# A one-core MoE decoder step: the transposes of one expert's activations moved into the next expert's up products, the first expert written out, and a re-ordered end

## The chip, the cores and the metric

The kernel runs on one core of a Trainium2 chip. The metric is the device time of one execution in microseconds (us); the time before is the median of three runs.

## The reference, cut to what matters

One decoder layer for a prompt of 256 tokens and 64 sample tokens (320 tokens, width 1024, float32). After the mixing part comes a mixture of 32 experts, four of them for each token, then a gated residual and a final RMS norm:

```python
def expert(args):
    xe, e = args
    hu = xe @ w_up[e] + b_up[e]                  # (slots, 1024) @ (1024, 2048)
    gate = jnp.minimum(hu[:, :D_FF], SWIGLU_LIMIT)
    lin = jnp.clip(hu[:, D_FF:], -SWIGLU_LIMIT, SWIGLU_LIMIT)
    glu = gate * jax.nn.sigmoid(SWIGLU_ALPHA * gate)
    return ((lin + 1.0) * glu) @ w_down[e] + b_down[e]   # (slots, 1024) @ (1024, 1024)
...
x = x + gt_f * moe(...)
y = rms_norm(x, g_final)
```

Each expert has 8 MB of up weights and 4 MB of down weights, and all 32 experts' weights have to come from HBM once.

## The kernel before

Each engine runs its own hand-ordered instruction list; semaphores join them (`S("name")`, `wait_ge`, `then_inc`). All on-chip data lies in one SBUF array `mem` and one PSUM array `psum` of 8 banks, so the profile shows those two names for nearly everything, and the lines tell the operations apart.

**Weights.** SyncE (SP) issues the loads. Up weights of an expert come as 4 pieces of 2 MB (`load_up`, L434) into 4 places, down weights as 4 pieces of 1 MB (`load_down`, L439) into 4 other places. There is one set of places for each kind, so a piece of expert e+1 can be issued once TensorE has counted up `piece_done` for that place with expert e. The order on the queue is: all of expert 0, up 1, and from then on up e, down e-1. The down weights of expert 31 (`load_last`, L452) go into the places of the up weights' first two pieces.

**TensorE (PE)**, in `expert(e)`, for each of the 32 experts in a hardware loop: the down products of expert e-2 (`down`, L1096; its bias L1076); the token counts of two experts read into registers; the up products of expert e over the 4 pieces (`up`, L1048; its bias L1052), in one of four sizes by token count (32, 64, 96 or 128 slots; `by_size`); the gather of expert e+1's tokens (L1008) into banks 4 and 5; the scatter of the outputs of expert e-2 for token tiles 0 and 1 (`scatter`, L1106); the transposes of expert e's activations (`turn_activations`, L1058) into banks 4 and 5, of which there are 2, 4, 6 or 8 by size; the transposes of the scatter weights (`turn_weights`, L1114) into bank 2; the scatter of tile 2. In the first two experts there is nothing to scatter, and 14 or 3 dummy products (`fill`, L517) stand in its place. `Pg` and `G` are the scatter weights before and after the transposes.

**VectorE (DVE)**: one-hot selectors for the next gather (L2143), the scatter weights (L2154), the gated activation in `swiglu` (L2172, L2173, L2176, L2179) into `gt_`, and the additions of the scattered outputs (L2205, counted by `added`). **ScalarE (ACT)**: the sigmoid (L1496), the copy of the gathered tokens (L1483), the copy of the turned weights (L1519), the copy of the turned activations into `actT` (L1510 to L1513) and of the down products into `yd` (L1530). **GpSimd (POOL)** picks the bias row (L1700, L1703).

Expert sizes in this data, in order of experts, as the counts of the L1052 and L1048 instructions show them: 96, 32, 32, 96, 64, 32, 64, 64, 32, 32, 64, 96, 64, 32, 64, 32, 32, 128, 32, 32, 32, 32, 32, 64, 64, 32, 64, 64, 32, 32, 64, 64.

**The end** (`last_expert` on PE and ACT, `finish` on DVE): down 30; transposes of expert 31's scatter weights (bank 1); down 31 in banks 6 and 7, whose start waits until ACT has copied expert 30's outputs out of those same banks (`y_copied`). Between the two halves of down 31 stand the scatter products of expert 30 (L1177, L1181). Then come the scatter products of expert 31 (sample tile L1188, prompt tiles L1193), the residual additions (L2230, L2232, L2235), per tile a sum of squares on ACT (L1546), two small steps on POOL (L1598, L1599), the scaling on DVE (L2240) and the store (L489). Tiles go in the order 2, 0, 1 (`LAST_ORDER`); the scalings all stand behind the additions of all tiles.

Of the kernel before, what the change touches and what calls it, by code (L numbers as in the profile page):

```python
# [13 lines left out]
D = 1024  # L14
# [71 lines left out]
def build(nc, a):  # L86
# [6 lines left out]
    with ctx:  # L93
# [128 lines left out]
        yd_last = at(2 * SLOT, 2, 512); G_last = at(2 * SLOT + D, NTOK)  # L222
        assert o5 + 7168 + 1536 <= WORDS, o5 + 8704
# [284 lines left out]
        def _(pe):  # L508
# [3 lines left out]

            def fill(n, bank):

                busy = at_bf(const_off["ones"], 256)
                for _ in range(n):
                    pe.matmul(psum[:, bank, 0:256], busy[:, 0:128], busy, start=True, stop=True)  # L517
# [466 lines left out]

            def gather_first():
# [13 lines left out]
                last.then_inc(S("gathered"), 1)  # L999

            def gather(i, count, turned, e=None):
# [12 lines left out]
                if count is None:  # L1014
                    products(128)
                    return
# [22 lines left out]
            def up(ig, it, slots):  # L1039
# [4 lines left out]
                for c in range(UP):  # L1044
                    pe.wait_ge(piece_in[c], 16 * (it + 1))
# [17 lines left out]
            def down(it, slots, meanwhile=None):  # L1063

                end = meanwhile is not None
# [9 lines left out]
                for u in range(2):  # L1075
                    pe.matmul(psum[0:slots, 6 + u, :], bsel_down[:, 0:slots],  # L1076
                              bparts[:, 2 * D + 512 * u:2 * D + 512 * u + 512], start=True, stop=False)
                last = [None] * DOWN
                for j in range(pieces):
                    if end and j == pieces // 2:  # L1080
                        meanwhile()
                    for u in range(2):
                        for q in range(tiles):
                            piece = q * pieces + j
                            c = piece // 2
                            if slots == 96:
                                turned = actT.rearrange("p j s -> p (j s)")[:, 0:8 * slots] \
                                    .rearrange("p (j s) -> p j s", j=KD)[:, piece, :]
                            else:
                                turned = actT[:, j, slots * q:slots * q + slots]  # L1090
# [5 lines left out]
                            last[c] = pe.matmul(psum[slots * q:slots * q + slots, 6 + u, :], turned,  # L1096
# [19 lines left out]

            def expert(e):
# [6 lines left out]
                by_size(pe, count, lambda slots: up(e, e, slots))  # L1124
# [24 lines left out]
            def expert_later(r, e, it, count_before):  # L1149
# [10 lines left out]
                turn_activations(it, SIZES[3])  # L1160
# [5 lines left out]
            def last_expert(its, count):  # L1166
# [3 lines left out]
                turn_weights(its, 1)  # L1170

                def scatter_before():

                    pe.wait_ge(S("G_ready"), its + 1)
                    pe.wait_ge(S("y_copied"), its + 1)
                    for u in range(2):
                        pe.matmul(psum[64 * u:64 * u + 64, 0, :], G[:, tok(2)], yd[:, u, :], start=True, stop=False)  # L1177
                    pe.wait_ge(S("y_gated"), 2)
                    for t in range(2):
                        for u in range(2):  # L1180
                            pe.matmul(psum[:, 2 + 2 * t + u, :], G[:, tok(t)], yd_gated[:, u, :], start=True, stop=False)  # L1181

                pe.wait_ge(S("y_copied"), its + 1)
# [1152 lines left out]
```

## Time and profile before

| | |
|---|---|
| median of 3 runs | 1298.41 us (1296.67 to 1298.94) |
| the profiled execution | 1295.37 us |
| its span, first to last instruction | 1293.6 us |
| PE busy | 1163.6 us (90%) |
| DVE, ACT, POOL busy | 375.8, 182.7, 72.0 us |
| data moved, mean rate | 467.36 MB, 361 GB/s |
| DMA queue of the weights (q1), share of 16 engines | 86.7% |
| mean granted TensorE clock | 0.970 |

PE is busy for 90% of the span and the DMA engines for 87%. Which of the two sets the time changes from stage to stage, so the shares alone do not say what an edit is worth. "Released" below means that the last product that reads a piece of weights is done.

### The profile page before, as it was taken

The numbers are of one execution on the slowest core, as the hardware profiler recorded it, in microseconds if no ns is written. First come the engines' busy times: TensorE is split into PE (matmuls) and PEld (weight loads), VectorE is DVE, ScalarE is ACT, GpSimd is POOL, SyncE is SP. The second block draws the span as 40 slices with busy tenths as digits, with TensorE's granted clock in tenths as the row PEclk, the third lists the DMA queues.
The fourth block names the chain that finished last, engine by engine and source line by source line (L and its number), as shares of the span: only waits on it lengthen the run. The fifth ranks groups of instructions, "written<-read, shape, count | busy, mean of one in ns | idle before, by whom it ended". The sixth has DMA issues, their size and how long they took to land.

```text
span 1293.6 us, 23349 instructions
## 1 busy us (share of the span) xinstructions
PE 1163.6 (90%) x8690; PEld 567.3 (44%) x8691; DVE 375.8 (29%) x819; ACT 182.7 (14%) x358; POOL 72.0 (6%) x178
## 2 busy tenths in 40 slices
PE   5999999996989999998999998999777889988986
PEld 4655447544335446443344544444223334343332
DVE  0164214848211222321222121142211221222235
ACT  3112232213010111110110110010100000110101
POOL 1010001431000000000000000000000000000001
PEclk9999999998899999998999999999879999989999
DMA  9944635883689999999999999999999999999992
GB/s 366 363 152 172 239 131 196 253 317 138 260 351 424 409 417 427 427 428 425 428 424 426 426 426 428 426 376 428 427 426 428 426 425 426 426 426 428 427 422 85
DMA packets 62481, 467.36 MB, mean 361 GB/s; under 512 B 6538, under 2 KB 24910, under 8 KB 26730
## 3 DMA queue, kind: packets, MB, share of 16 engines
q1 hardware_dynamic: 59770, 461.86, 86.7%
q10 hardware_dynamic: 2288, 4.37, 1.1%
q0 software_dynamic: 384, 0.59, 0.2%
q8 instruction: 28, 0.46, 0.1%
q14 instruction: 11, 0.09, 0.0%
HBM read 459.78 MB, written 6.42 MB: 360 GB/s over the span
## 4 chain that ended last, share of the span: by engine, by line
PE 58%; DMA 36%; DVE 2%; issue 2%; ACT 1%; POOL 0%; SPq 0%; ACTq 0%; POOLq 0%; DVEq 0%
DMA mem<-in_w_up 33%; PE psum L1048 20%; PE psum L1096 9%; PE psum L680 6%; PE psum L1106 5%; PE psum L661 3%; PE psum L1008 3%; PE psum L867 2%; PE psum L684 2%; DMA mem<-in_in_chunks 1%; PE psum L536 1%; DMA mem<-in_mod_chunks 1%; PE psum L1058 1%; PE psum L871 1%; PE psum L1052 1%
## 5 line engine op out<-in xcount | busy, mean ns | idle before, releaser
L1048 PE MATMUL psum<-mem 128*32 128x512 f32 (+2 forms) x2432 | 399.9, 628 | 74.0 <-DMA mem<-in_w_up 66.8
L1048 PEld LDWEIGHTS psum<-mem 128*32 128x32 f32 (+2 forms) x2432 | 133.7, 123 | 330.3 <-issue 203.4
L1096 PE MATMUL psum<-mem 128*32 128x512 f32 (+3 forms) x1024 | 207.8, 594 | 0.0
L2172 DVE TENSOR_SCALAR mem<-psum 128x256 f32<-128x256 f32 (+3 forms) x32 | 19.2, 601 | 542.6 <-PE psum L1052 542.6
L1106 PE MATMUL psum<-mem 128*128 128x512 f32 x360 | 143.1, 608 | 3.3 <-DVE mem L2173 2.2
L1096 PEld LDWEIGHTS psum<-mem 128*32 128x32 f32 (+3 forms) x1024 | 93.3, 127 | 87.4 <-issue 61.2
L2205 DVE TENSOR_TENSOR mem<-mem,psum 128x1024 f32<-128x1024 f32 (+1 forms) x90 | 94.1, 1045 | 95.8 <-PE psum L1106 95.8
L680 PE MATMUL psum<-mem 128*128 128x512 f32 x192 | 84.2, 595 | 0.0
L1008 PEld LDWEIGHTS psum<-mem 128*128 128x128 bf16 x2232 | 74.7, 99 | 19.4 <-issue 19.1
L1496 ACT ACTIVATE mem<-mem 128x256 f32<-128x256 f32 (+3 forms) x32 | 17.9, 561 | 451.0 <-DVE mem L2172 451.0
L1008 PE MATMUL psum<-mem 128*128 128x64 bf16 (+1 forms) x2232 | 78.4, 196 | 0.0
L1106 PEld LDWEIGHTS psum<-mem 128*128 128x128 f32 x360 | 49.0, 171 | 51.9 <-issue 47.3
L1700 POOL CAST mem<-mem 128x128 bf16 (+1 forms) x33 | 10.7, 324 | 937.5 <-PE psum L1096 894.2
L680 PEld LDWEIGHTS psum<-mem 128*128 128x128 f32 x192 | 36.0, 190 | 43.7 <-issue 43.6
L2143 DVE TENSOR_SCALAR mem<-mem 128x128 bf16<-128x128 f32 (+1 forms) x99 | 22.2, 281 | 69.2 <-issue 69.2
L1513 ACT COPY mem<-psum 128x256 f32<-128x256 f32 (+2 forms) x29 | 14.0, 484 | 189.1 <-PE psum L1096 189.1
L661 PE MATMUL psum<-mem 128*128 128x320 f32 x128 | 36.7, 447 | 2.1 <-DMA mem<-in_in_chunks 2.1
L1246 ACT COPY mem<-psum 128x320 f32<-128x320 f32 (+9 forms) x65 | 25.0, 395 | 95.4 <-PE psum L680 68.1
L1519 ACT COPY mem<-psum 128x320 f32<-128x320 f32 x32 | 13.7, 428 | 155.9 <-PE psum L1106 147.7
L536 PE MATMUL psum<-mem 128*32 128x128 f32 x768 | 25.0, 286 | 7.8 <-DMA mem<-in_mod_chunks 6.9
L1530 ACT COPY mem<-psum 128x1024 f32<-128x1024 f32 x31 | 31.5, 1018 | 0.0
L661 PEld LDWEIGHTS psum<-mem 128*128 128x128 f32 x128 | 25.0, 197 | 13.1 <-DMA mem<-in_in_chunks 2.2
(279 smaller groups left out, 803.4 us busy)
## 6 DMA issues: line engine op xcount, KB each, us to landing
mem<-in_w_up SPq DMA_DIRECT2D x128, 2048.0 KB, 22.3
mem<-in_w_down SPq DMA_DIRECT2D x128, 1024.0 KB, 15.9
mem<-in_mod_chunks SPq DMA_DIRECT2D x12, 2048.0 KB, 12.3
mem<-in_in_chunks SPq DMA_DIRECT2D x8, 2048.0 KB, 9.9
mem<-in_out_chunks SPq DMA_DIRECT2D x2, 2048.0 KB, 10.0
mem<-in_x_prompt ACTq DMA_DIRECT2D x2, 1024.0 KB, 6.9
mem<-in_state_ret SPq DMA_DIRECT2D x4, 512.0 KB, 8.7
mem<-in_state_mlstm_c SPq DMA_DIRECT2D x4, 512.0 KB, 7.7
```

Of the source, the lines that this page charges most:

```text
L536: last = pe.matmul(psum[32 * t:32 * t + 32, bank, 0:128], cT[:, k, :], w[:, k, 128 * t:128 * t + 128], start=(k == 0), stop=False)
L661: last = pe.matmul(psum[:, q % BANKS, 0:NTOK], w[:, k, 128 * m:128 * m + 128], hT[:, k, :], start=(k == 0), stop=(k == KD - 1))
L680: last = pe.matmul(psum[:, q % BANKS, :], hT[:, k, tok(t)], w[:, k, :], start=(k == 0), stop=(k == KD - 1))
L684: last = pe.matmul(psum[64 * u:64 * u + 64, q % BANKS, 0:256], hT[:, k, tok(t)], w[:, k, 256 * u:256 * u + 256], start=(k == 0), stop=(k = ...
L867: last = pe.matmul(psum[:, 6 + u, :], hT[:, k, tok(t)], w[:, k, :], start=(k == 0), stop=(k == KD - 1))
L1008: last = pe.matmul(psum[:, 4 + k // 4, 128 * (k % 4):128 * (k % 4) + slots], h2p[:, part, t, dealt(k)], P[:, t, 0:slots], start=(part == 0 ...
L1048: last = pe.matmul(out, xg[:, 2 * c + h, cols], moving, start=(c + h == 0), stop=False)
L1096: last[c] = pe.matmul(psum[slots * q:slots * q + slots, 6 + u, :], turned, place(c, 2, D)[:, piece % 2, 512 * u:512 * u + 512], start=(j = ...
L1106: last = pe.matmul(out, G[:, tok(t)], yd[:, u, :], start=True, stop=True)
L1246: act.copy(*pairs[-1]).then_inc(S("evacuated"), 1)
L1530: act.copy(yd.rearrange("p u n -> p (u n)"), flat(6, D)).then_inc(S("y_copied"), 1)
L2205: TT(v, v, src, ALU.add).then_inc(S("added"), 1)
```

## The change

1. `turn_activations` moves. The transposes of expert e-1's activations are now issued inside expert e's `up`, ahead of its fourth piece, and there are always 8 of them, whatever the size. Counts of `act_ready` and `act_turned` start one higher. ACT copies them out behind the copies of the turned weights and of the down products, one expert later than before. The gather of expert e+1 waits for that copy (`actT_ready`), as banks 4 and 5 are shared.
2. The first expert (`expert_first`) is written out ahead of the loop, which now runs from 1. Its counts are read into registers in `gather_first`, ahead of the last 8 gather products. The dummy products `fill` are gone.
3. Expert 31's activations are turned between the loop and down 30, and ACT copies them into a buffer of their own (`actT_last`, in the place of up piece 2). Down 31 goes to banks 4 and 5 and runs in one piece; it no longer waits for `y_copied`. The scatter products of expert 30 stand behind it, and prompt tile 1 is multiplied after tile 0 is finished, into banks 6 and 7.
4. On DVE the scalings are put between the additions: add tile 0, scale tile 2, add tile 1, scale tile 0, scale tile 1. The load of the final norm's gains is issued before down 31 is done.

```diff
             def gather_first():
...
                     for t in range(NT):
+                        if part == 2 and t == NT - 1:
+                            pe.wait_ge(S("counts_ready"), 1)
+                            first_counts = count_at(1), count_at(2)
                         pe.wait_ge(S(f"part{part}"), t + 1)
...
-            def up(ig, it, slots):
+            def up(ig, it, slots, turn_before=False):
...
                 for c in range(UP):
+                    if turn_before and c == UP - 1:
+                        turn_activations(it - 1)
                     pe.wait_ge(piece_in[c], 16 * (it + 1))
...
-            def turn_activations(it, slots):
-                pe.wait_ge(S("act_ready"), it + 1)
-                for j in range(KD * slots // 128):
+            def turn_activations(it):
+                pe.wait_ge(S("act_ready"), it + 2)
+                for j in range(KD):
...
+            def expert_first(count, count_next):
+                by_size(pe, count, lambda slots: up(0, 0, slots))
+                gather(1, count_next, 1)
+                pe.wait_ge(S("gate_ready"), 1)
+                pe.wait_ge(S("lin_clipped"), 1)
+                pe.nop().then_inc(S("scattered"), 1)
+                pe.nop().then_inc(S("scattered"), 1)
+                pe.wait_ge(S("added"), 1 + CLEARED)
+                turn_weights(0, 2)
+                pe.nop().then_inc(S("scattered"), 1)
...
-                by_size(pe, count, lambda slots: up(e, e, slots))
+                by_size(pe, count, lambda slots: up(e, e, slots, True))
                 gather(e + 1, count_next, e + 1, e)
...
                     pe.nop().then_inc(S("scattered"), 1)
                     pe.nop().then_inc(S("scattered"), 1)
-                    with pe.If(e < 1):
-                        fill(14, 6)
-                    with pe.Else():
-                        fill(3, 6)
-                pe.wait_ge(S("xg_ready"), e + 3)
-                by_size(pe, count, lambda slots: turn_activations(e, slots))
                 pe.wait_ge(S("added"), 3 * e + 1 + CLEARED)
                 turn_weights(e, 2)
...
             def last_expert(its, count, acts):
...
+                by_size(pe, count, lambda slots: down(its - 1, slots, True, acts))
+                pe.wait_ge(S("G_ready"), its + 1)
+                pe.wait_ge(S("y_copied"), its + 1)
...
+                samples(G, yd, True)
+                pe.wait_ge(S("y_gated"), 2)
+                prompt(0, G, yd_gated, True)
                 pe.wait_ge(S("G_ready"), its + 2)
+                samples(G_last, yd_last, False).then_inc(S("last_scattered"), 1)
                 pe.wait_ge(S("y_gated"), 4)
+                prompt(0, G_last, yd_last_gated, False).then_inc(S("last_scattered"), 1)
+                prompt(1, G, yd_gated, True)
+                prompt(1, G_last, yd_last_gated, False).then_inc(S("last_scattered"), 1)
...
-            with pe.Fori(0, NE) as e:
+            expert_first(*gather_first())
+            with pe.Fori(1, NE) as e:
                 expert(e)
+            turn_activations(NE - 1)
             by_size(pe, count_at(NE - 1), lambda slots: down(NE - 2, slots))
...
# ACT
             def expert(r, e, it, count, count_next):
                 take_up(r * (NE + 1) + e, it, count, count_next)
                 copy_weights(it)
-                by_size(act, count, lambda slots: copy_turned(it, slots, True))
+                down_before(it)
+                act.copy(yd.rearrange("p u n -> p (u n)"), flat(6, D)).then_inc(S("y_copied"), 1)
+                by_size(act, count, lambda slots: copy_turned(it, slots, actT))
...
# DVE, finish
+                add_last(0)
+                dve.wait_ge(S("gfin_in"), 16)
+                scale(0)
+                add_last(1)
+                scale(1)
+                scale(2)
```

## Rows read from the trace of the kernel before

**Rows 1.** The page: rate of the DMA in 40 slices of the span

```profile
GB/s 366 363 152 172 239 131 196 253 317 138 260 351 424 409 417 427 427 428 425 428 424 426 426 426 428 426 376 428 427 426 428 426 425 426 426 426 428 427 422 85
```

**Rows 2.** The chain that ended last, late in the loop: start, us, what

```profile
1214.78 3.68 PE psum L1048 x16
...
1244.30 3.65 PE psum L1048 x16
```

**Rows 3.** Windows: length, busy per engine, PEclk, DMA share, GB/s

```profile
308.00:332.00 24.00, 18.02 (x154) 9.95 (x158) 14.91 (x44) 8.05 (x11) 0.00 (x0) 0.78 0.01 3
...
355.00:360.00 5.00, 4.21 (x35) 2.44 (x37) 0.85 (x3) 1.20 (x3) 0.00 (x0) 0.88 0.07 29
440.00:442.00 2.00, 1.91 (x9) 0.65 (x10) 0.85 (x3) 1.49 (x3) 0.60 (x2) 1.00 0.43 94
856.00:860.00 4.00, 4.00 (x41) 1.10 (x35) 1.59 (x6) 1.93 (x2) 0.53 (x2) 1.00 0.26 55
```

**Rows 4.** SP's queue: first issues of weight loads behind the first two pauses

```profile
331.92 33.39 SPq L434 DMA_DIRECT2D mem<-in_w_up  x8
...
359.87 5.45 SPq L434 DMA_DIRECT2D mem<-in_w_up  x4
```

**Rows 5.** Timeline, from the first gather to the first up products

```profile
317.61 0.62 PE L996 MATMUL psum<-mem 128*128 128x128 bf16 x8 [0.22 <-DVE mem L2089]
...
318.27 0.69 DVE L2255 COPY mem<-psum 128x512 f32<-128x512 f32 x1 [0.72 <-PE psum L996]
...
321.81 0.87 PE L1048 MATMUL psum<-mem 128*32 128x512 f32 x1 [3.58 <-issue]
324.24 22.64 PE L1048 MATMUL psum<-mem 128*32 128x512 f32 x188 [1.56 <-issue]
```

**Rows 6.** Windows around the first products, for the granted clock (PEclk)

```profile
318.00:322.00 4.00, 0.42 (x6) 0.17 (x3) 2.92 (x13) 1.87 (x2) 0.00 (x0) 1.00 0.03 8
...
324.00:329.00 5.00, 4.76 (x24) 1.16 (x28) 2.51 (x7) 0.00 (x0) 0.00 (x0) 0.51 0.02 5
...
353.00:356.00 3.00, 3.00 (x16) 2.39 (x15) 0.67 (x3) 0.00 (x0) 0.00 (x0) 0.50 0.65 273
```

**Rows 7.** Timeline from the end of up 0 to behind up 1

```profile
350.86 0.96 DVE L2179 TENSOR_TENSOR mem<-mem 128x768 f32<-128x768 f32 x1
352.49 2.94 PE L517 MATMUL psum<-mem 128*128 128x256 bf16 x14 [2.31 <-issue]
...
357.72 7.07 PE L1048 MATMUL psum<-mem 128*32 128x512 f32 x64 [0.79 <-ACT mem L1519]
...
367.98 0.50 PE L517 MATMUL psum<-mem 128*128 128x256 bf16 x3 [0.76 <-issue]
```

**Rows 8.** The chain that ended last: the activations of a 128-slot expert turned

```profile
851.40 0.95 PE psum L1058 x8
```

**Rows 9.** The same chain from down 30 on

```profile
1255.79 7.14 PE psum L1096 x31
...
1265.29 0.38 PE psum L1076
...
1269.32 0.86 PE psum L1177 x4
1270.18 3.63 PE psum L1181 x8
...
1278.58 1.48 PE psum L1188 x4
...
1281.52 1.22 DVE mem L2232
...
1284.02 1.16 ACT mem L1546 x2
...
1287.08 1.28 POOL mem L1598
...
1289.03 1.29 DVE mem L2240
```

More of the change, by code:

```diff
@@ L983, in _, with count_at @@
             turn_rows(2)
+            def count_at(i):
+                where = slice(i, i + 1) if isinstance(i, int) else bass.ds(i, 1)
+                return pe.value_load(counts_i[0:1, where], min_val=0, max_val=NTOK)
             def gather_first():
@@ L1015, in gather @@
                     products(128)
+                    return
+                if e is None:
+                    with pe.If(count <= 64):
+                        products(64)
+                    with pe.Else():
+                        products(128)
                     return
@@ L1061, in turn_activations, with down @@
                 last.then_inc(S("act_turned"), 1)
-            def down(it, slots, meanwhile=None):
-                end = meanwhile is not None
+            def down(it, slots, end=False, acts=actT):
+                first = 4 if end else 6
                 def place(c, *shape):
@@ L1095, in down @@
                                     pe.wait_ge(piece_in[UP + c], 16 * (it + 2))
-                            last[c] = pe.matmul(psum[slots * q:slots * q + slots, 6 + u, :], turned,
+                            last[c] = pe.matmul(psum[slots * q:slots * q + slots, first + u, :], turned,
                                                 place(c, 2, D)[:, piece % 2, 512 * u:512 * u + 512],
@@ L1164, in expert_later, with last_expert @@
                 by_size(pe, count_before, lambda slots: down(it - 1, slots))
-            def last_expert(its, count):
+            def last_expert(its, count, acts):
                 pe.wait_ge(S("G_ready"), its + 1)
@@ L1170, in last_expert, with samples @@
                 turn_weights(its, 1)
-                def scatter_before():
-                    pe.wait_ge(S("G_ready"), its + 1)
-                    pe.wait_ge(S("y_copied"), its + 1)
+                by_size(pe, count, lambda slots: down(its - 1, slots, True, acts))
+                pe.wait_ge(S("G_ready"), its + 1)
+                pe.wait_ge(S("y_copied"), its + 1)
+                def samples(weights, rows, first):
                     for u in range(2):
[L1177 to L1181, printed above, removed]
@@ L1183, in last_expert, with prompt @@
-                pe.wait_ge(S("y_copied"), its + 1)
-                by_size(pe, count, lambda slots: down(its - 1, slots, scatter_before))
+                        if not first:
+                            pe.wait_ge(S("y_copied"), its + 2 + u)
+                        last = pe.matmul(psum[64 * u:64 * u + 64, 0, :], weights[:, tok(2)], rows[:, u, :],
+                                         start=first, stop=not first)
+                    return last
+                def prompt(t, weights, rows, first):
+                    for u in range(2):
+                        last = pe.matmul(psum[:, (2, 6)[t] + u, :], weights[:, tok(t)], rows[:, u, :],
+                                         start=first, stop=not first)
+                    return last
@@ L1185, in last_expert @@
+                samples(G, yd, True)
+                pe.wait_ge(S("y_gated"), 2)
+                prompt(0, G, yd_gated, True)
                 pe.wait_ge(S("G_ready"), its + 2)
-                for u in range(2):
-                    pe.wait_ge(S("y_copied"), its + 2 + u)
-                    last = pe.matmul(psum[64 * u:64 * u + 64, 0, :], G_last[:, tok(2)], yd_last[:, u, :], start=False, stop=True)
-                last.then_inc(S("last_scattered"), 1)
+                samples(G_last, yd_last, False).then_inc(S("last_scattered"), 1)
@@ L1190, in last_expert @@
                 pe.wait_ge(S("y_gated"), 4)
-                for t in range(2):
-                    for u in range(2):
-                        last = pe.matmul(psum[:, 2 + 2 * t + u, :], G_last[:, tok(t)], yd_last_gated[:, u, :], start=False, stop=True)
-                    last.then_inc(S("last_scattered"), 1)
+                prompt(0, G_last, yd_last_gated, False).then_inc(S("last_scattered"), 1)
+                prompt(1, G, yd_gated, True)
+                prompt(1, G_last, yd_last_gated, False).then_inc(S("last_scattered"), 1)
@@ L1562, in _ @@
             copy_weights(0)
-            by_size(act, count, lambda slots: copy_turned(0, slots, False))
             act.nop().then_inc(S("y_copied"), 1)
-            with act.Fori(1, NE) as e:
+            by_size(act, count, lambda slots: copy_turned(0, slots, actT))
+            with act.Fori(1, NE - 1) as e:
                 expert(0, e, e, count_at(e + 1), count_at(e + 2))
@@ L2246, in _ @@
             dve.nop().then_inc(S("added"), CLEARED)
+            dve.nop().then_inc(S("act_ready"), 1)
             dve.memset(counts[:, 0:1], 0.0)
```

67 lines of the change are left out of this document (34 added, 33 removed).

## The prediction

> **What bounds the kernel now.** I read the page first. Its rate row [rows 1] is ragged over the first 12 of 40 slices, which are the mixing part that the change does not touch. From slice 13 on (about 390 us) it stands at 409 to 428 GB/s but for one slice, the 376 of slice 27. That is a stream of weights which hardly pauses, so in the expert part the time is that of the DMA stream: its start, its pauses, and what is left to do when it has ended.
>
> The chain that ended last says the same late in the loop [rows 2]: TensorE starts the products on an expert's fourth up piece at 1214.78 and on the next one's at 1244.30, 29.5 us later, and between them stands the landing of weights. 12.58 MB in 29.5 us is 426 GB/s, the full rate. An edit inside such an iteration is worth nothing as long as TensorE is back in time.
>
> Then I looked for the pauses of the stream [rows 3]. There are four behind the last piece of expert 0's weights: 308 to 332 (24 us, 3 GB/s), 355 to 360 (29 GB/s instead of 426, so 4.7 us lost), 440 to 442 (94 GB/s, 1.6 us lost) and 856 to 860 (55 GB/s, 3.5 us lost). In each the queue had nothing to do because TensorE had not released a piece. The first ends at the issue of 331.92, when the first piece of expert 0 is released, the second at 359.87, with the first piece of expert 1 [rows 4]. These two are what parts 1 and 2 of the change can reach. Behind up 31 the stream has only the last down weights to bring, and the end is a chain of PE, DVE, ACT and POOL [rows 9], which parts 3 and 4 reach.
>
> **Part A, the start of up 0.** The last 8 gather products start at 317.61, and DVE's copy of the tokens ends at 318.27 + 0.69 = 318.96. The first up product starts only at 321.81, 2.85 us later, with "issue" as releaser, and the second at 324.24, behind another 1.56 us of "issue" [rows 5]. In the first gap stand two register loads, the entry of the loop, a branch, and the choice of size. The change takes the loads and the loop entry out of it. No row prices them apart. From below: the branches and jumps alone make up the gap, gain 0; indeed the loads may hold back the last 8 gather products, which had only 0.22 us of waiting. From above: all 2.85 us. I take 1.5. The second gap I leave as it is, for the same products stand behind the same kind of branch.
>
> The gap has a second price. The granted clock is 1.00 over 318 to 322 and 0.51 over 324 to 329 [rows 6], 1.2 instead of 2.4 GHz, after TensorE had been busy for 0.42 of 4.00 us. 24 products in 4.76 us at the low level are about 2.4 us more than they take at the high one. With the idle shortened to about 2 us before the first product, whether the clock falls is open: it was still full at 322. I count half, 1.2 us (ends: 0 and 2.4). Part A gives 1.5 + 1.2 = 2.7 us (0 to 5.3), and as the queue waits for this very release, the stream is earlier by all of it.
>
> **Part B, from up 0 to the first release of up 1.** Before, TensorE waits 2.31 us for "issue", runs 14 dummy products, turns and reaches up 1 at 357.72 [rows 7]. Now the dummies and the turn are gone. What must be waited for is `added`, which DVE counts behind its last activation step, at 350.86 + 0.96 = 351.82. With half a microsecond for the three weight transposes that is done near 352.6 (three at the 0.12 of [rows 8], and a handover). From there it could go on at once, but now the loop is entered, with code that has not run yet: the same loop entry, two loads and choice of size that part A sheds. By the gap of part A, 2.85 us, up 1 starts at 355.5, 2.2 us earlier than before. But the dummies were what kept TensorE at work: even with them the clock was at 0.50 over 353 to 356 [rows 6], and it was back in time for up 1 at 357.72. Without them up 1 meets the low level, and its first piece (a quarter of the 7.07 us of [rows 7], 1.77 us) takes 3.54. So the release comes at 359.0 instead of 359.5: gain 0.5. Bounds: with an entry of no cost up 1 starts 5.1 earlier, less the 1.8 of the clock, +3.3; with the second gap of 1.56 us too, -1.1, taken as -1.5.
>
> The Trainium skill (TensorE: Matmul & The Clock Gate, the part on the clock gate) calls the low clock the default and says that it is activity which lifts it; it speaks against taking the dummy products away. The row of 353 to 356 agrees. If the clock never fell, part B would be 2.2 us instead of 0.5.
>
> **Part C, the turn inside the up products.** Work moves and grows: always 8 transposes where there were size / 16. 8 take 0.95 us [rows 8], 0.12 us each. Over 16 experts of 32 slots, 12 of 64 and 3 of 96 that is 96 + 48 + 6 = 150 more, 18 us in all. They cost nothing where TensorE waits for the fourth piece anyway, as it does wherever the pattern of [rows 2] holds: the third piece's products, 3.68 at 64 slots, and 0.95 us fit into the 4.9 us between two pieces. If that cover went, each would cost its 0.12.
>
> It counts where TensorE leads, from up 1 on, and the pause at 440, which ends with a down piece released in expert 4, measures it. Up to there 8 turns each come into up 1, 2 and 3: +2.85. Behind up 1 go a gap of 0.76 and 3 dummies of 0.50 [rows 7]; behind up 1, 2 and 3 go 2 + 2 + 6 turns, 1.2. That is 2.85 - 0.76 - 0.50 - 1.2 = +0.4, and the pause grows by it: loss 0.5 (0, where it is hidden, to 2, if ACT's copy of the turned activations also holds up the gather; the fourth piece's products, 1.77 us and more, cover it otherwise). What is queued behind `act_ready` on TensorE is the rest of the up products, but the activations are ready an iteration before. The pause at 856 has one turn of 0.95 moved from behind the products to inside them, hence no change.
>
> **Part D, the end.** All of it hangs on the landing that starts the products at 1244.30. 8 transposes instead of 4 before down 30: +0.5. Down 30 ended at 1255.79 + 7.14 = 1262.93, and down 31 waited for ACT's copy until 1265.29 [rows 9]. Now it follows the weights' transposes: 1262.93 + 0.5 + 0.5, and 0.8 for the choice of size, as in the gap of 0.76 [rows 7]: 1264.8, gain 0.5. It runs in one piece, 0.38 + 7.14 = 7.5 us like down 30, to 1272.3. Then come the samples of expert 30 (0.86) and prompt tile 0 (half of 3.63, 1.81), and the second samples start at 1275.0. Before, L2232 started 1281.52 - 1278.58 = 2.94 behind that point; so now at 1277.9, ending at 1279.2. Scaling tile 2 waits for 1.16 on ACT and 0.8 to 1.95 on POOL; with 0.8 it runs 1281.2 to 1282.5. Prompt tile 1's 3.63 us of products end at 1281.3, so its addition, like L2232 some 1.22, runs 1282.5 to 1283.7. Its square takes 1.16. From the start of POOL's last step to that of the last scaling lie 1289.03 - 1287.08 = 1.95, and the scaling takes 1.29: 1288.1, with handovers 1288.3. Before it ended at 1289.03 + 1.29 = 1290.3. Gain 2.0 (1.0 if down 31 gains nothing and the handovers cost 0.5 more; 3.2 if POOL's last step is as short as 0.7). What is late next is POOL behind the last square.
>
> **Sum.** 2.7 + 0.5 - 0.5 + 2.0 = 4.7 us. The profiled execution took 1295.37 us, of which 1293.6 are the span; it would take 1290.7. The median of the three runs, 1298.41, lies 3.0 above the profiled one, and I carry the difference over: 1293.7.
>
> **The rivals.**
> *The start gives nothing back.* Part A's gap is branches and jumps, the clock falls as before, and the new loop entry eats part B. Then A is 0, B is 0 and the rest 1.5: 1296.9. For it: "issue" is named for the whole gap, no load is seen in it. Against: the same branches cost 2.31 us at 352.49 without a register load and 0.76 an iteration later [rows 7], so a gap is not of one size, and the loads' share of 2.85 is not nothing.
> *The clock stays up.* With shorter idle both times, TensorE is at 2.4 GHz in up 0 and up 1: A is 3.9 to 5.3, B 2.2, D 2.0, less 0.5: about 8 us, 1290.4. For it: the full level at 318 to 322. Against: the fall at 353 after only 2.3 us of idle.
> *Slower: the loop is met cold.* Written out, the first expert warms none of the loop's code, so the entry cost is paid twice: both gaps of [rows 5], 2.85 + 1.56, fall between 352.6 and the second product of up 1, and the rest of up 1 and its 8 transposes run at the low level. First release 357.0 + 3.54 = 360.9, a loss of 1.4; the rest of up 1 loses 3 us more, which all go into the pause at 440, with 2 of part C at its upper bound; A gives 0 and the end 2.0. Loss 4.4: 1302.8. It decides when up 1's first release is later than 361 and the pause at 440 longer than 5 us. Against: up 1 is the first of size 32, so its code ran for the first time at 357.72 too, as one group of 64 without a gap [rows 7].
> The Trainium skill (Runtime: NRT & Kernel Launch, instruction fetch mechanics) says that a taken branch whose target is not in the engine's present window makes it fetch, and stall. By that rule this last rival's two gaps would come. No row here names a fetch.
>
> **How the numbers follow.** The case of the sum has 0.50, the start that gives nothing 0.24, the clock that stays up 0.18, the cold loop 0.08. A change of 0.2%, 2.6 us, is about what a measurement of this kernel can tell from none. The first case runs from 1290.5 to 1297.0, mostly beyond 2.6 us, with 0.05 of its 0.50 inside; the second lies within it; the third is faster. The cold loop splits 0.07 slower and 0.01 same. Faster 0.63 and, with 0.04 of the second case that gains over 2.6 by the end alone, 0.67; same 0.26; slower 0.07. The range leaves out the cold loop and the outer halves of the others: 1289.5 to 1297.8.
>
> **What would show each step.** A: the first up product near 320.3, the issue at 331.92 now near 329.2. B: the second issue near 356.7 (359.87 less 0.5 and A), the granted clock at half when up 1 starts. C: 8 turns ahead of each fourth piece, the pause at 440 about 0.5 longer, 29.5 us from fourth piece to fourth piece unchanged. D: 44.0 us from the fourth piece's products of expert 31 to the end of the last scaling, instead of 1290.3 - 1244.3 = 46.0. The whole would be wrong if a new pause of the stream appears between 440 and 560, or if the gather waits for ACT.

## The result, and the profile after

The changed kernel takes 1309.82 us (median of 4 runs, 1308.26 to 1312.82), the kernel before beside it 1298.55 (4 runs, 1296.67 to 1298.94): a ratio of 1.0106, 95% interval 1.0083 to 1.0129. It is 11.3 us slower; the prediction had 4.7 us faster and a range that ended at 1297.8. The profiled execution took 1308.91 us, its span 1307.1, which is 13.5 us more than before.

The rate row of the page answers to [rows 1]:

```profile
GB/s 368 368 136 190 216 130 195 291 278 138 265 255 385 377 416 405 425 426 429 427 426 426 401 428 423 427 393 428 426 427 427 427 427 425 424 426 426 426 425 146
```

Slices 12 to 14, about 359 to 457 us, were at 351, 424 and 409 GB/s; now they are at 255, 385 and 377. The loss is there, at the start of the expert part. To the right of it the row is nearly what it was.

The timeline of TensorE from the first gather on answers to [rows 5, 7]: start, us, what, and in brackets the idle time ahead of it and what ended it.

```profile
318.08 0.62 PE L998 MATMUL psum<-mem 128*128 128x128 bf16 x8 [0.37 <-issue]
319.69 20.81 PE L1059 MATMUL psum<-mem 128*32 128x512 f32 x192 [0.99 <-DVE mem L2295]
340.28 0.86 PE L1063 MATMUL psum<-mem 128*32 128x512 bf16 x12
341.07 2.28 PE L1011 MATMUL psum<-mem 128*128 128x64 bf16 x72
345.19 0.62 PE L1124 MATMUL psum<-mem 128*128 128x128 f32 x3 [1.84 <-DVEq L2227]
352.86 7.33 PE L1059 MATMUL psum<-mem 128*32 128x512 f32 x48 [7.05 <-issue]
360.12 1.22 PE L1070 MATMUL psum<-mem 128*128 128x128 f32 x8
361.27 1.93 PE L1059 MATMUL psum<-mem 128*32 128x512 f32 x16
363.01 0.40 PE L1063 MATMUL psum<-mem 128*32 128x512 bf16 x4
369.49 1.25 PE L1011 MATMUL psum<-mem 128*128 128x64 bf16 x20 [6.07 <-issue]
374.71 2.88 PE L1011 MATMUL psum<-mem 128*128 128x64 bf16 x52 [3.98 <-issue]
381.41 0.96 PE L1124 MATMUL psum<-mem 128*128 128x128 f32 x3 [3.82 <-issue]
383.83 1.06 PE L1088 MATMUL psum<-mem 128*96 128x512 bf16 x2 [1.46 <-issue]
```

Up 0 (L1059 here is L1048 of before) starts 0.99 us behind the gather and runs as one group of 192: both gaps of [rows 5] are down to this one. Then, from the moment the loop is entered at expert 1, there are five waits named "issue" (the engine waited for nothing that the profile shows), 7.05 + 6.07 + 3.98 + 3.82 + 1.46 = 22.4 us. One of them, the 3.98, stands in the middle of 72 gather products that have nothing between them but each other. Before, the same stretch (from the end of expert 1's gather to down 0) held 2.31 + 0.76 and some 2 us more, of which 1.74 stood ahead of down 0:

```profile
371.43 0.60 PE L1076 MATMUL psum<-mem 128*96 128x512 bf16 x2 [1.74 <-issue]
```

So the last of the five waits, 1.46, is not new; the other four are new or several times longer.

The queue of the weight loads answers to [rows 4]:

```profile
325.09 38.64 SPq L435 DMA_DIRECT2D mem<-in_w_up  x8
389.90 10.63 SPq L440 DMA_DIRECT2D mem<-in_w_down  x4
...
356.72 4.00 SPq L435 DMA_DIRECT2D mem<-in_w_up  x3
```

(The last line is from a closer window, within the group of 8.) The first release is at 325.09 instead of 331.92, 6.8 us earlier; expert 1's first is at 356.72 instead of 359.87, 3.2 us earlier; but the first down piece of expert 0 is at 389.90, where it was 375.64. In 33 us TensorE went from 3.2 us ahead to 14.3 us behind. Windows answer to [rows 3, 6] (columns as there):

```profile
318.00:322.00 4.00, 2.94 (x32) 1.42 (x36) 2.88 (x13) 1.87 (x2) 0.00 (x0) 1.00 0.02 4
324.00:329.00 5.00, 5.00 (x52) 1.86 (x48) 2.89 (x7) 0.00 (x0) 0.00 (x0) 1.00 0.58 180
353.00:356.00 3.00, 3.00 (x16) 0.65 (x17) 0.00 (x0) 0.00 (x0) 0.00 (x0) 0.50 0.00 0
...
378.00:389.00 11.00, 6.13 (x12) 2.61 (x13) 1.28 (x6) 0.65 (x2) 0.00 (x0) 0.69 0.06 22
450.00:460.00 10.00, 9.64 (x59) 3.72 (x60) 3.84 (x9) 1.44 (x2) 0.53 (x2) 1.00 0.58 216
```

The granted clock stays at its upper level in up 0 (52 products in 5.00 us where there were 24 in 4.76) and is at the lower one at the start of up 1. The stream stands from 378 to 389 (22 GB/s) and runs at half its rate between 450 and 460 (216 GB/s, 4.9 us lost).

The chain that ended last, late in the loop and from the last up piece on, answers to [rows 2, 8, 9]:

```profile
1232.64 3.68 PE psum L1059 x16
...
1262.18 3.65 PE psum L1059 x16
...
1272.99 1.15 PE psum L1070 x8
...
1282.14 0.33 PE psum L1088
...
1292.33 1.03 PE psum L1195 x4
...
1294.81 1.23 DVE mem L2262
...
1301.90 0.19 POOL mem L1628
...
1302.76 1.29 DVE mem L2272
```

Fourth piece to fourth piece is 29.5 us, unchanged. Expert 31's fourth piece is met at 1262.18, 17.9 us later than before. From there to the end of the last scaling it takes 1304.05 - 1262.18 = 41.9 us instead of 46.0, so the new end gives 4.1 back: 17.9 - 4.1 = 13.8, close to the span's 13.5. The stream's own account gives the 17.9: expert 1's release came 3.2 us earlier; at 427 GB/s the 137 GB/s over 378 to 400 are 14.9 us lost; and from 400 to 1240 us it loses 13.2 us instead of 7.3. That is 14.9 + 5.9 - 3.2 = 17.6.

### The profile page after: what moved, and what is told of

It is laid out like the page before. It is cut to its first block, busy times and chain, and to the rows that moved or that the text cites. A ratio compares the mean times of both kernels' runs of the same rounds, so it can differ in the third digit from the quotient of the medians.

```text
span 1307.1 us, 23471 instructions
## 1 busy us (share of the span) xinstructions
PE 1179.1 (90%) x8821; PEld 582.9 (45%) x8824; DVE 375.7 (29%) x819; ACT 184.8 (14%) x357; POOL 70.7 (5%) x178
## 4 chain that ended last, share of the span: by engine, by line
PE 61%; DMA 32%; issue 3%; DVE 2%; ACT 1%; POOL 0%; SPq 0%; ACTq 0%; POOLq 0%; DVEq 0%
DMA mem<-in_w_up 30%; PE psum L1059 20%; PE psum L1106 10%; PE psum L675 6%; PE psum L1116 5%; PE psum L1011 3%; PE psum L656 3%; PE psum L862 2%; DMA mem<-in_mod_chunks 2%; PE psum L679 2%; PE psum L1070 1%; PE psum L531 1%; PE psum L1124 1%; PE psum L1088 1%; PE psum L866 1%
## 5 line engine op out<-in xcount | busy, mean ns | idle before, releaser
L1059 PE MATMUL psum<-mem 128*32 128x512 f32 (+2 forms) x2432 | 391.8, 611 | 57.6 <-DMA mem<-in_w_up 48.1
L1059 PEld LDWEIGHTS psum<-mem 128*32 128x32 f32 (+2 forms) x2432 | 125.9, 122 | 293.6 <-issue 199.1
L1106 PEld LDWEIGHTS psum<-mem 128*32 128x32 f32 (+3 forms) x1024 | 97.7, 128 | 83.8 <-issue 52.0
L1116 PEld LDWEIGHTS psum<-mem 128*128 128x128 f32 x360 | 50.0, 171 | 50.8 <-issue 44.3
L675 PEld LDWEIGHTS psum<-mem 128*128 128x128 f32 x192 | 36.0, 190 | 43.7 <-issue 43.6
L1070 PEld LDWEIGHTS psum<-mem 128*128 128x128 f32 x256 | 33.7, 208 | 27.6 <-issue 27.6
L1070 PE MATMUL psum<-mem 128*128 128x128 f32 x256 | 39.8, 300 | 0.0
L1511 ACT ACTIVATE mem<-mem 128x256 f32<-128x256 f32 (+3 forms) x32 | 17.9, 560 | 141.3 <-DVE mem L2202 141.3
```

The source lines that it names most:

```text
L675: last = pe.matmul(psum[:, q % BANKS, :], hT[:, k, tok(t)], w[:, k, :], start=(k == 0), stop=(k == KD - 1))
L1059: last = pe.matmul(out, xg[:, 2 * c + h, cols], moving, start=(c + h == 0), stop=False)
L1070: last = pe.transpose(flat(4, D)[:, 128 * j:128 * j + 128], gt_.rearrange("p u (w i h) -> p u w h i", w=2, h=2)[:, j // 4, j // 2 % 2, j % ...
L1106: last[c] = pe.matmul(psum[slots * q:slots * q + slots, first + u, :], turned, place(c, 2, D)[:, piece % 2, 512 * u:512 * u + 512], start= ...
L1116: last = pe.matmul(out, G[:, tok(t)], yd[:, u, :], start=True, stop=True)
```

## The experiments

Theory 1 (theory F in the first expectations): the loop's code has to be fetched when it is first run. With the first expert inside the loop, part of those fetches fell into the 22 us of up 0; with the first expert written out they fall into expert 1, which is short. Rivals: the moved turn, the missing dummy products with the clock, and, for the size of a single wait, the weights' traffic that the fetch shares the DMA engines with.

**Only the first expert written out.** The kernel before, dummies and old turn kept, counts read behind the first gather as before:

```diff
+            expert_first(count_at(1), count_at(2))
-            with pe.Fori(0, NE) as e:
+            with pe.Fori(1, NE) as e:
```

> The kernel before with one edit: the first expert is written out ahead of the loop, dummies and turn kept as they were. Theory F (first fetch under load: TensorE's loop code runs for the first time while the weights stream, and each wait for code takes 4 to 7 us instead of 1.5): long 'issue' gaps behind up 0, 15 us and more in sum between 345 and 395, and the time 10 to 18 us over the kernel before. Rival T (the 8 transposes inside the up products make TensorE late): no change, within 3 us of the kernel before. Rival L (the low clock without the dummies): no change either, as the dummies are kept.

Measured: 1308.66 us (6 runs), ratio 1.0097 (1.0066 to 1.0129), 12.9 us over the kernel before on that chip (1295.72). Its timeline has 5.08 us of "issue" ahead of up 1, 4.00 and 5.64 around the gather, 1.67 and 4.14 at the dummies, 1.44 ahead of down 0, and down 0's first release at 390.37. So this one edit makes the whole loss, with the dummies in place. Its register loads still stand behind the first gather, and yet up 0 starts 1.18 us behind it, where the kernel before needs 3.58.

**Everything but that.** The changed kernel with the loop from 0, counts read in the loop, no `expert_first`, and `bsel_ready` waited for ahead of the turn:

```diff
-            expert_first(*gather_first())
-            with pe.Fori(1, NE) as e:
+            gather_first()
+            with pe.Fori(0, NE) as e:
```

> The changed kernel with the loop running from 0 again, its first expert inside it (which turns data that nobody uses in up 0; the counts are read in the loop). Turn and end stay changed, no dummies. Theory F: the gaps behind up 0 shrink to under 5 us in sum; only the turns' cost and the end's 4 us remain, so 1294 to 1300. Rivals T and L: the time stays near 1309.

Measured: 1296.19 us (10 runs), ratio 1.0003 (0.9979 to 1.0028). The waits are back near their old size (2.85 us ahead of up 1, 0.73 ahead of the weights' transposes, 1.73 ahead of down 0), and the start is slow again: 5.85 us ahead of up 0. Down 0's release is at 377.90.

**Only the rebuilt end.** The kernel before with parts 3 and 4 of the change; the turn of expert 31 stays in the loop, ACT copies it to `actT_last`:

```diff
-                last_expert(NE, count_at(NE))
+                last_expert(NE, count_at(NE), actT_last)
```

> The kernel before with the rebuilt end alone (own buffer and banks, tile by tile; 4 transposes of expert 31 in the loop as before). From the fourth up piece of expert 31 to the last scaling 46.0 us became 41.9 in the changed kernel. Expected by every theory: that gain alone, some 4.5 us (4 transposes fewer than in the changed kernel), 1293 to 1295; if instead the end only moved with the rest, no change.

Measured: 1290.62 us (10 runs), ratio 0.9950 (0.9929 to 0.9971), 5.1 us faster. From expert 31's fourth piece to the end of the last scaling it takes 41.1 us instead of 46.0. Between this kernel and the one before it lie the moved turn and the missing dummies: 5.6 us.

**The stream held ahead of expert 1.** Is a fetch slow because weights are moving? In the changed kernel SP waits ahead of expert 1's up pieces until TensorE is inside the loop's `up`:

```diff
+            sp.wait_ge(S("entered"), 1)
             load_ups(1, 1)
```

> The changed kernel, but SyncE holds back the four up pieces of expert 1 until TensorE has entered up 1 inside the loop, so that nothing streams while the loop is entered. Theory F: the gap ahead of up 1 (7.05 us of 'issue') shrinks: up 1's code is reached within 3 us of the end of the weight transposes, seen at the issue of the first piece. A rival to it, B (the number of branches and loads alone makes the gap): 7 us from the weight transposes to that issue. The time itself is longer by either, since the stream starts 20 us later.

Measured once: 1322.46 us. Nothing moved while the loop was entered, and TensorE got from the weights' transposes (end 347.2) to the count in `up`, just ahead of the first product, by 350.9: 3.7 us, nearer to theory F's 3 than to the rival's 7. The changed kernel's 7.05 reach further, to the product itself, which here waits for its weights. But the pieces then landed beside the later waits:

```profile
381.98 1.14 PE L1012 MATMUL psum<-mem 128*128 128x64 bf16 x18 [6.24 <-issue]
387.76 3.06 PE L1012 MATMUL psum<-mem 128*128 128x64 bf16 x54 [4.64 <-issue]
394.93 0.95 PE L1127 MATMUL psum<-mem 128*128 128x128 f32 x3 [4.10 <-issue]
397.33 1.06 PE L1091 MATMUL psum<-mem 128*96 128x512 bf16 x2 [1.44 <-issue]
```

The third falls where the stream was already drying up (60 GB/s over 392 to 395), so this run decided nothing on what traffic does to the later waits. The place of the hold was badly chosen: it left the traffic on most of the waits that were to be tested.

**The stream held ahead of expert 2.** The same, one line later, until TensorE has come through the loop's first pass:

```diff
             load_ups(1, 1)
+            sp.wait_ge(S("entered"), 1)
             with sp.Fori(2, NE) as e:
```

> The changed kernel, but the weight queue waits ahead of expert 2's up pieces until TensorE has come to the end of the loop's first pass (expert 1). So TensorE meets the loop's code while no weights are moving. In the changed kernel three waits named issue lie in that stretch: 6.07 us at 363.4, 3.98 us in the middle of the gather, 3.82 us ahead of the weights' transposes, 13.9 us together. Theory 1, code met for the first time costs its fetch whatever else moves: the three stay at 10 us or more together, and the stream starts again near 383, 26 us later than it did: about 1335 us. Theory 2, a fetch is slow only because it shares the DMA engines with the weights: the three shrink to under 6 us together, the stream starts again near 375, about 1327 us.

Measured: 1303.09 us in one run, then in 10 more 1304.57, ratio 1.0059 (1.0040 to 1.0078), where the changed kernel has 1.0106. Both numbers expected for the time were far too high: I had let the held pieces be 20 us late for expert 2, and they are not, since TensorE is at down 0 when they land. Timeline and window of the first run:

```profile
364.90 1.25 PE L1012 MATMUL psum<-mem 128*128 128x64 bf16 x20 [3.76 <-issue]
367.30 2.96 PE L1012 MATMUL psum<-mem 128*128 128x64 bf16 x52 [1.16 <-issue]
371.78 0.62 PE L1125 MATMUL psum<-mem 128*128 128x128 f32 x3 [1.52 <-issue]
374.36 1.02 PE L1089 MATMUL psum<-mem 128*96 128x512 bf16 x2 [1.96 <-issue]
```

```profile
356.00:371.00 15.00, 9.34 (x120) 5.83 (x112) 2.18 (x7) 1.89 (x4) 0.00 (x0) 0.77 0.03 5
```

The same four waits are 8.4 us instead of 15.3, and the three that the forecast named 6.4 instead of 13.9, nearer to theory 2's 6 than to theory 1's 10. The first two show it cleanly: with 5 GB/s moving instead of 420 (363 to 375 us in the changed kernel) they are 4.9 us instead of 10.1. The third, 1.52 instead of 3.82, is less clear, since in the changed kernel the stream was already drying up beside it (128 GB/s over 377 to 382, most of that in the first 2 us); the fourth did not shrink (1.96, and 1.46 there). As 2.7 us of waiting stood in this stretch before the change too, code met first costs 5 to 6 us here without traffic. The changed kernel has about 7 more; 5 of them are in the first two waits and are the traffic's. The wait ahead of up 1 has expert 1's pieces beside it in both kernels, and stays at 6.84. The second set of runs had 3.49, 1.48, 1.03 and 1.62 for the four, 7.6 us.

Its expectation, written before the second set:

> The changed kernel with the stream held back during the loop's first pass, once more with rounds: it was 1303.1 us in one run, 6 us under the changed kernel, with the named waits of the first pass 8.4 us instead of 15.3. Theory 1 (a fetch waits behind the weights' transfers, which costs about as much again as the fetch): ratio 1.003 to 1.007. Theory 2 (chance of one run): 1.008 to 1.012, as the changed kernel.

**The second expert written out too.**

```diff
             expert_first(*gather_first())
+            expert_second(count_at(2), count_at(3))
-            with pe.Fori(1, NE) as e:
+            with pe.Fori(2, NE) as e:
```

> The changed kernel with the second expert written out as well, the loop from 2. Theory 1, each piece of code costs its fetch when it is first run, and a short expert (32 slots) has no long products to hide it: the written second expert shows gaps like those of the changed kernel's first pass through the loop, and the loop's first pass shows them once more: 10 us or more of new gaps, of which the stream may cover a part, 1314 to 1324 us. Theory 2, the gaps are a single cost of going into a loop from code ahead of it, wherever that is: the gaps move one expert later and the time stays within 3 us of 1309.8.

Measured: 1314.51 us (4 runs), ratio 1.0133 (1.0108 to 1.0157). The chain has the waits in the written expert 1 and once more in the loop's first pass, at expert 2:

```profile
364.64 5.89 issue
370.53 2.57 PE psum L1011 x45
373.10 4.03 issue
...
406.62 11.86 issue
418.49 1.57 PE psum L1011 x13
```

So it is each copy of the code that costs, and most of it not the step into a loop. The wait ahead of up 1 is the exception: 7.05 us where up 1 is reached by entering the loop, 1.33 (ended by ACT) where expert 1 is written out and its code follows on. The DMA section of the page counts the fetches of that queue: queue, kind, packets, MB, share. First the changed kernel, then this one.

```profile
q8 instruction: 32, 0.52, 0.2%
```

```profile
q8 instruction: 37, 0.61, 0.2%
```

Packets of 16 KB each. The kernel before has 28, as have all the kernels here with one copy of the expert; with the first expert alone written out and the old end it is 33, five more. The changed kernel, whose copy has no dummies and no turn, has four more than its twin with the loop from 0, and the second copy adds five. (That q8 is TensorE's is read from this count: in the second of the pair nothing else has grown.) Between 317 us and down 0 the changed kernel has 11 of them, the kernel before 6 (both counted in windows of the DMA view), and none of the loop's comes again after its first pass. Such packets start inside or just ahead of each of the long waits: at 348 and 351 us ahead of up 1, at 364.9 and 365.5, at 372, at 378. In the kernel before, those of 325 and 338 start under the products of up 0, that of 349 under the gather and that of 355 under the dummies and the turn, where no wait shows them. A packet is itself under way for only 0.9 to 2.1 us, so most of a wait of 4 to 6 us is not the transfer. With the stream held, the two packets behind up 1 took no less time (1.85 and 2.09 us, against 1.13 and 2.03) but started 1.1 us ahead of the wait instead of 1.5 us into it; what the traffic delays is thus at least in part their start.

**Without the dummies.** The rebuilt end, old turn, no `fill`:

```diff
-                    with pe.If(e < 1):
-                        fill(14, 6)
-                    with pe.Else():
-                        fill(3, 6)
```

> The kernel before with the rebuilt end, and without the dummy products in the first two experts; the turn of the activations stays where it was. The rebuilt end alone took 1290.6 us; with the turn moved and no dummies and the loop from 0 it was 1296.2. Theory 1, the moved turn accounts for the 5.6 us: this kernel takes 1289 to 1292. Theory 2, the dummies kept the clock and covered work, and their loss accounts for it: 1294 to 1297.

Measured: 1292.78 us (11 runs), ratio 0.9974 (0.9960 to 0.9987): between the two theories, 1 to 3 us over the rebuilt end alone (0.9950 and, later, 0.9961), though the intervals overlap. Up 1 shows a likely cause: 64 products in 9.77 us at the lower clock, where they take 7.07 with dummies ahead.

**The turn alone.** The changed kernel with the loop from 0 and the dummies kept, beside the rebuilt end alone on one chip. (The edit is that of "Everything but that", and the lines of `fill` back in.)

> The changed kernel with the loop from 0 and with the dummy products kept, so that it differs from the kernel before only in the moved turn and the rebuilt end. Theory 1, the moved turn costs 3 to 5 us by itself (8 transposes of 1.15 us in each expert where TensorE leads or lags, and gaps ahead of the down products): with the rebuilt end's 5 us gained it comes out near the kernel before, 1294 to 1297 us, and above the rebuilt end alone, which runs beside it. Theory 2, it was the missing dummies and the fallen clock at expert 1 that cost it: 1290 to 1292 us, as the rebuilt end alone.

> The kernel before with the rebuilt end alone once more, on the same chip as the three others of this set, as their measure. It had a ratio of 0.995; both theories expect 0.993 to 0.997 again.

Measured: 1295.87 us (12 runs), ratio 0.9986 (0.9966 to 1.0006), against 1291.50 (12 runs), 0.9961 (0.9942 to 0.9980). The medians are 4.4 us apart, as theory 1 of these expectations has it; the intervals overlap by a little, so that the size rests on the medians and the traces. The view of TensorE's waits over 395 to 1240 us (us in all, times, longest), first with the turn moved, then with the rebuilt end alone:

```profile
PE psum L1063 <- DMA mem<-in_w_up: 43.4, 34, 3.0
PE psum L1092 <- issue: 12.0, 29, 0.7
```

```profile
PE psum L1049 <- DMA mem<-in_w_up: 67.8, 42, 3.0
PE psum L1077 <- issue: 3.0, 8, 0.5
```

TensorE's slack against the stream falls by 24 us of 68, and the choice of size ahead of the down products is now waited for in 29 experts instead of 8. Counted from the rate in windows of 10 us against 427 GB/s, the stream loses 11.5 us between 400 and 1240 with the turn moved, and 6.7 without; 9.0 and 4.8 in the pair without dummies. The pause at 440 is not where it goes in the pair with dummies (2.7 us in both).

**Loop entered early.** An attempt at a better version: the rebuilt end, and the last 8 gather products put inside the loop, so that it is entered and the counts are read while TensorE waits for VectorE.

```diff
                 count, count_next = count_at(e + 1), count_at(e + 2)
+                with pe.If(e < 1):
+                    gather_part(2, NT - 1).then_inc(S("gathered"), 1)
+                with pe.Else():
+                    pe.nop()
                 by_size(pe, count, lambda slots: up(e, e, slots))
```

> The kernel before with the rebuilt end, and the last 8 products of the first gather moved into the loop, behind the counts and ahead of the up products, under a branch for e < 1. The loop is entered and the counts are read while TensorE waits for VectorE anyway. Theory 1 (the start's gap is loop entry and register loads, and the loop's code is fetched once in this form): up 0 starts some 2 us earlier, the clock stays up, first release near 327 instead of 332, 1284 to 1288 us. Theory 2, the gap is the choice of size alone, or the branch costs as much anew: 1289 to 1292 us, as the rebuilt end alone.

> The rebuilt end with the last 8 gather products inside the loop, once more, beside the rebuilt end alone on one chip. Its trace had expert 0's first down piece released 55.9 us behind the first gather, against 58.1 with the rebuilt end alone. Theory 1, this goes through to the end: ratio 0.991 to 0.995, 1 to 3 us under the rebuilt end. Theory 2, it is given back at the pauses behind 440 and at 850, where TensorE and not the stream sets the time: within 1 us of it or above it.

Measured: 1293.00 us (12 runs), ratio 0.9971 (0.9954 to 0.9989), and in the second set 1292.24, 0.9969 (0.9950 to 0.9988), beside 0.9961 for the rebuilt end alone. The first up product still starts 3.32 us behind the gather, so loads and loop entry alone do not make that gap; the second gap is gone, and from the gather's end to down 0's release it takes 55.9 us instead of 58.1. Those 2 us do not reach the end: in the window of 850 to 860 us, where the 128-slot expert makes TensorE the bound, the stream loses 3.8 and 4.3 us, against 1.8 (and 3.1 one window later) with the end alone. Whether that is all of it stays open.

The rebuilt end alone remains the fastest kernel, 0.4 to 0.5% under the kernel before.

## Why the prediction was wrong

**The step that failed is part B**: "the loop is entered, with code that has not run yet: the same loop entry ... By the gap of part A, 2.85 us". It priced one entry. What first-run code costs is not an entry but a fetch for every 16 KB of it: 6.57 us in the chain ahead of up 1, and then 6.07, 3.98 and 3.82 us on the way to down 0, beside the 1.46 that is no longer than before. The forecast for the second release, 356.7, was met (356.72), and by accident: part A gave 4 us more than I had, and part B took 3.7 (from first to second release 31.6 us instead of 28.0) where I had it give 0.5. And I stopped the sum there. From the second release to down 0's, 33.2 us have become of 15.8: 12.6 of the 17.4 are the "issue" waits (15.3 against 2.7 before), the rest the turn of 1.2 and products that ran at the lower clock after the waits (the gather 4.1 instead of 2.3; from down 0's first product to its release 6.1 instead of 4.2). The window of 378 to 389 is my "new pause of the stream", only earlier than where I looked for it.

**The rival named for this, "the loop is met cold", had the mechanism and a fifth of its waits, and its time, 1302.8, was still 7 us short.** (By its own terms it comes to 0.4 less: 357.0 + 3.54 is 360.5, not 360.9.) Its sign, a first release later than 361, did not show, since part A's gain hid the loss. It took both gaps of [rows 5] as the whole price, 4.4 us, because those were the only cold gaps on the page. The rest of the same code was met under work, 22 us of up 0, the gather and the dummies, as the packets' starts show: covered, not free. I priced the edit by what showed, and did not ask what up 0 had been covering. I gave it 0.08; my reason against it ("up 1 is the first of size 32, so its code ran for the first time at 357.72 too ... without a gap") mistook code that had not run for code that had not been brought: the loop's last packet there starts at 355, ahead of up 1's 357.72. The Trainium skill (Runtime: NRT & Kernel Launch, instruction fetch mechanics) says of a taken branch outside the present window that its page must be fetched before execution goes on. The run with two written experts agrees for code met first behind a choice of size (5.89 and 11.86 us, with packets starting in both); its 4.03 us stand between two products without a branch, and that rule does not give them. The section's further statement that only two blocks are held does not fit: the six or seven blocks met in the loop's first pass run to the end of the loop with no further packet (none between 382 and 1280 us). The 128 KiB that it also gives for TensorE, eight blocks by my estimate from its 16 KiB, would hold them.

**Part A** came out with the right sign and too small: 6.8 us instead of 2.7. From the end of DVE's copy (319.44 in the chain) to the first up product it takes 0.25 us instead of 2.85; the second gap, which I left as it was, went as well (1.56); the clock never fell, which gives the first piece's products 3.1 us; and the gather started 0.5 later: 2.6 + 1.6 + 3.1 - 0.5 = 6.8. But the reason given for it, that loads and loop entry leave the gap, is not borne out: with both moved away the gap was 3.32 and 4.25 us. Nor do the loads matter where the first expert is written out: left behind the gather, they leave 1.18 us. In the kernel before, instruction packets start in both gaps (318.9 and 321.9 us), so the gap was more likely in part the same fetch, and the written-out expert spared it because its code follows on directly; that was not tested by itself.

**Part C** was mis-sized: 0.5 us forecast, 3 to 4.4 measured (difference of the ratios, of the medians). A turn of 8 takes 1.15 us, not 0.95; the choice of size ahead of `down` is now waited for, 9 us more in 29 gaps, by my reading because the old turn's products had stood ahead of it; and "they cost nothing where TensorE waits for the fourth piece anyway" holds only in experts with that much slack. In the changed kernel pauses show in the windows of 10 us from 450 (4.9 us), 490, 730 and 870; the kernel before has them from 440 and 850. The missing dummies, counted in part B at 1.77 us of clock, cost 1 to 3 in the medians, likely by that same clock; the intervals of the pairs with and without them overlap.

**Part D** came out with the right sign and too small: 2.0 us forecast, 4.1 in the changed kernel, 5.1 and 4.8 alone in medians. Down 31 starts 20.0 us behind the fourth piece (forecast 20.5). From POOL's last step to the last scaling it takes 0.9 us instead of 1.95, and the samples' addition starts 2.5 us behind their products' start instead of 2.9. (The reading that the rate stands at 409 to 428 GB/s from slice 13 on, but for one slice, passes over the last slice, 85, which is this end.)

By experiment the two halves of the change add up: the first expert written out 1.0097 and the rest 1.0003 give 1.0100, against 1.0106 measured.

## What to carry to other kernels

Code that is run for the first time has a price for each block, and it is seen only where no long work covers it: before writing an iteration out ahead of a loop, ask what the loop's first pass was hidden under, and count the instruction packets. An edit that adds work "where the engine waits anyway" is to be checked against the smallest slack, not the usual one. An edit at the very end of the chain is worth its full size; one at the start can be given back wherever another engine sets the time later.

## What was not expected of the hardware

- Every further copy of the expert's code added four or five instruction packets of 16 KB (28, 32 or 33, 37), and the first pass through code that nothing covers held 12 to 22 us of waits, while each packet itself took 0.9 to 2.1 us.
- The wait for such code is longer while weights stream: two waits of 10.1 us together at 420 GB/s were 4.9 with the stream held, and holding it back made the kernel 5 to 6 us faster (1.0059 against 1.0106, on different chips).
- A wait of this kind can stand between two products of one straight run, with no branch between them (20 and 52 of 72, or 45 and 27 with another copy ahead): its place moves with the amount of code ahead of it.
